# Strassen pairs in nine of eleven iterations of an up projection, with the token sums moved and the residual's row added by transfers

## The reference, cut to what matters

```python
def conv_ffn(x, w_up, b_up, w_dw, b_dw, w_down, b_down):
    h = x @ w_up + b_up                       # 1024 -> 2 * 2816
    h = causal_depthwise_conv(h, w_dw, b_dw)  # width 3
    g, val = jnp.split(h, 2, axis=-1)
    return (jax.nn.silu(g) * val) @ w_down + b_down

y = conv_ffn(x, ...)
x = layer_norm(DEEPNORM_ALPHA * x + y, norm2_g[i], norm2_b[i])   # alpha = 2 ** 0.5
```

## Time and profile before

| | before |
|---|---|
| median of 3 runs | 1028.91 us (1028.56 to 1029.22) |
| the profiled execution, its own time | 1028.89 us |
| its span, first to last instruction | 1027.0 us |
| PE busy | 1010.0 us (98%), 5091 matmuls |
| DVE busy | 839.9 us (82%) |
| ACT busy | 586.2 us (57%) |
| POOL busy | 285.3 us (28%) |
| mean granted clock of PE | 0.997 |

### The profile page before, as it was taken

The page is one execution under the profiler, slowest core; times in us unless marked ns, Lnnn a source line. Parts: engine busy times, 40 slices in busy tenths (PEclk is TensorE's granted clock), DMA queues, the critical chain, the costliest instruction groups (busy, mean ns, idle before and its releaser), DMA issues.

```text
span 1027.0 us, 14802 instructions
## 1 busy us (share of the span) xinstructions
PE 1010.0 (98%) x5091; PEld 853.8 (83%) x5091; DVE 839.9 (82%) x1154; ACT 586.2 (57%) x869; POOL 285.3 (28%) x321
## 2 busy tenths in 40 slices
PE   8999999999999999999999999999999999999997
PEld 6777788988899888888888888898888988888885
DVE  6999977698988688687895869769988867768888
ACT  6898864455665555565453443345656554456553
POOL 2988830594243100000020200049433400000001
PEclk9999999999999999999999999999999999999999
DMA  9766269379999722376555333827989963327653
GB/s 306 242 164 164 60 146 336 129 192 216 276 210 271 200 98 82 125 264 206 198 168 200 126 107 111 307 66 200 243 266 224 256 171 101 103 87 265 201 191 117
DMA packets 64440, 189.85 MB, mean 185 GB/s; under 512 B 7424, under 2 KB 8448, under 8 KB 63872
## 3 DMA queue, kind: packets, MB, share of 16 engines
q1 hardware_dynamic: 44144, 137.76, 39.6%
q0 software_dynamic: 18224, 44.05, 21.5%
q10 hardware_dynamic: 2016, 7.34, 2.1%
HBM read 178.11 MB, written 54.53 MB: 227 GB/s over the span
## 4 chain that ended last, share of the span: by engine, by line
PE 74%; DVE 10%; ACT 3%; issue 2%; DMA 1%; POOL 0%; DVEq 0%; POOLq 0%; ACTq 0%
PE ps L1981 11%; PE ps L1979 11%; PE ps L1980 11%; PE ps L2270 6%; PE ps L2272 6%; PE ps L2271 6%; PE ps L1989 4%; PE ps L1990 4%; PE ps L1991 4%; PE ps L2219 3%; PE ps L2221 3%; PE ps L2220 3%; DVE ps L1584 2%; DVE wl L1279 1%; DVE wl L1573 1%
## 5 line engine op out<-in xcount | busy, mean ns | idle before, releaser
L1979 PE MATMUL ps<-xh,wh 128*128 128x512 f32 x656 | 258.1, 394 | 0.6 <-DVE wl L1279 0.6
L1980 PE MATMUL ps<-xl,wh 128*128 128x512 f32 x656 | 255.4, 389 | 0.0
L1981 PE MATMUL ps<-xh,wl 128*128 128x512 f32 x656 | 255.3, 389 | 0.0
L784 ACT ACTIVATE wh<-raw 128x1024 fp32r<-128x1024 f32 x114 | 119.9, 1057 | 81.9 <-PE ps L2272 63.0
L1279 DVE TENSOR_TENSOR wl<-raw,wh 128x1024 fp32r<-128x1024 f32 x101 | 127.8, 1271 | 40.5 <-ACT wh L784 40.5
L1979 PEld LDWEIGHTS ps<-xh,wh 128*128 128x128 f32 x656 | 123.2, 188 | 27.2 <-issue 1.2
L1980 PEld LDWEIGHTS ps<-xl,wh 128*128 128x128 f32 x656 | 123.2, 188 | 26.1 <-issue 1.2
L1981 PEld LDWEIGHTS ps<-xh,wl 128*128 128x128 f32 x656 | 123.1, 188 | 25.8
L596 POOL TENSOR_SCALAR veps<-sqs 128x1 f32<-128x1 f32 x15 | 5.7, 383 | 496.7 <-ACT squares_down L978 377.4
L1573 DVE TENSOR_TENSOR wl<-raw,wh 128x1024 fp32r<-128x1024 f32 x70 | 89.4, 1277 | 23.6 <-ACT wh L1022 23.6
L2270 PE MATMUL ps<-wh,parts 128*128 128x512 f32 x264 | 102.7, 389 | 0.0
(11 more groups left out here) (269 smaller groups left out, 2205.6 us busy)
## 6 DMA issues: line engine op xcount, KB each, us to landing
raw<-d_weights SPq DMA_DIRECT2D x156, 512.0 KB, 4.3
raw<-summed SPq DMA_DIRECT2D x56, 512.0 KB, 4.1
summed<-d_weights POOLq DMA_DIRECT2D x88, 256.0 KB, 9.9
summed<-d_weights SPq DMA_DIRECT2D x66, 256.0 KB, 5.2
summed<-summed POOLq DMA_DIRECT2D x46, 256.0 KB, 5.6
wl<-raw POOLq DMA_DIRECT2D x4, 1024.0 KB, 7.2
wl<-raw POOLq DMA_DIRECT2D x5, 512.0 KB, 7.4
xraw<-d_x_fm SPq DMA_DIRECT2D x8, 256.0 KB, 7.1
```

Of the source, the lines that this page charges most:

```text
L784: eng.activation(split_at(u)[0], raw[:, u % RAW, :], ACT.Copy).then_inc(w_hi, 1)
L1979: eng.matmul(ps[:, bank, cols], a, xh[:, k, cols], start=(k == 0), stop=False)
L1980: eng.matmul(ps[:, bank, cols], a, xl[:, k, cols], start=False, stop=False)
L1981: mm = eng.matmul(ps[:, bank, cols], b, xh[:, k, cols], start=False, stop=(k == KD - 1))
```

## The change

- Strassen iterations are 1 to 9 instead of 2 to 6, in both layers. Iterations 0 and 10 stay regular. `first_strassen` moves from iteration 1 to iteration 0.
- The token sums move from rows 7 to 10 of all eight slots to rows 2 to 9 of four slots (`T_SLOTS`), those of the split hidden tiles. Those splits are put off: the regular iteration 0 and the Strassen iterations only make `n5` (`difference`), and iteration 10 splits rows 0 to 4 and 5 to 9 in two blocks of each of two tensors (`highs` on ACT, `lows` on DVE, 1280 columns each) and makes `s2` in two blocks (`sums_of`).
- The second two `token_parts` of the first Strassen iteration come behind its first `started` and `taps`.
- The early units and the normalisation's scratch tiles move to other slots.
- The residual of the feed-forward parts: ACT divides the bias row by ALPHA (in the first slot of iteration 0), POOL adds it to the four residual tiles by accumulating transfers behind `summed_weights`, and the first additions of the down projection multiply by ALPHA. `residual` on DVE stays in the gated MLP alone.

```diff
-S_FROM, S_TO = 2, 7
+S_FROM, S_TO = 1, 10
+T_SLOTS = (0, 1, 3, 6)
+S_ROWS, TF_ROWS, TH_ROWS = slice(0, 2), slice(2, 6), slice(6, 10)
+CHUNKS = (slice(0, S_TO // 2), slice(S_TO // 2, S_TO))
...
             summed_weights(layer)
+            eng.wait_ge(br_ok, layer + 1)
+            for t in range(NT):
+                eng.dma_start(res[:, t, :], brow[:, :], accum_op=ALU.add).then_inc(res_add, 16)
...  (ACT)
+            def highs(c):
+
+                ahead(KQ - 1, c)
+                if c == 1:
+                    eng.wait_ge(pr, 2 * S_TO + layer * KH)
+                if c in (1, 2):
+                    rows = CHUNKS[c - 1]
+                    for h, f in ((a11h, a11), (a12h, a12)):
+                        eng.activation(h[:, rows, :], f[:, rows, :], ACT.Copy).then_inc(h_hi, S_TO // 2)
+
-            regular(0, lambda c: his([u0 + c + LEAD] if c else []), in_banks)
             regular(S_FROM - 1, first_strassen, in_banks)
             strassen(S_FROM, True, lambda: token_parts((3, 2)))
             with eng.Fori(S_FROM + 1, S_TO - 1) as i:
                 strassen(i, True)
             strassen(S_TO - 1, False)
...
+            regular(KQ - 1, highs, in_sbuf, True)
...  (DVE)
+            def difference(i):
+
+                eng.wait_ge(pr, i * 2 + (layer * KH + 2))
+                eng.tensor_tensor(n5[:, bass.ds(i, 1), :], a21[:, bass.ds(i, 1), :], a22[:, bass.ds(i, 1), :],
+                                  ALU.subtract).then_inc(a_sum, 1)
+
+            def low(i, q):
+
                 eng.wait_ge(h_hi, i * 2 + (q + layer * KH + 1))
...
+            def lows(k):
+
+                rows = CHUNKS[k]
+                eng.wait_ge(h_hi, layer * KH + S_TO * (k + 1))
+                for l, f, h in ((a11l, a11, a11h), (a12l, a12, a12h)):
+                    eng.tensor_tensor(l[:, rows, :], f[:, rows, :], h[:, rows, :].bitcast(f32), ALU.subtract).then_inc(h_lo, S_TO // 2)
...
+                    product(i, q, accs)
+                    if last:
+                        low(i, q)
+                difference(i)
...
+            def last_tiles(c):
+
+                ahead(KQ - 1, c)
+                if c in (1, 2):
+                    lows(c - 1)
+                if c == 3:
+                    eng.wait_ge(h_lo, layer * KH + S_TO)
+                    sums_of(0, S_TO // 2, S_TO)
+
+            regular(KQ - 1, last_tiles, in_sbuf, True)
+            eng.wait_ge(h_lo, (layer + 1) * KH)
+            sums_of(S_TO // 2, KQ, S_TO // 2 + KQ)
...
-                    add(0, 0, p1, 1.0)
-                    add(1, 0, p1 + 1, 1.0)
+                    eng.wait_ge(res_add, 16 * NT * (layer + 1))
+                    add_first(0, p1)
+                    add_first(1, p1 + 1)
...  (PE)
-                eng.wait_ge(h_lo, layer * KH + max(2 * i + 1, 2 * (S_TO + 1)))
+                eng.wait_ge(h_lo, layer * KH + max(2 * i + 1, 2 * S_TO))
```

More of the change, by code:

```diff
@@ L210, in build_trunk @@
     a22h, a22l = slot_of(parts, 6), slot_of(parts, 7)
[L212 to L221, removed]
+    sum4h, sum4l, v2h, v2l = [parts[:, i, S_ROWS, :].rearrange("p k n -> p (k n)") for i in T_SLOTS]
+    t_f = [made[:, i, TF_ROWS, :] for i in T_SLOTS]
+    t_l = [parts[:, i, TF_ROWS, :] for i in T_SLOTS]
+    t_h = [parts[:, i, TH_ROWS, :] for i in T_SLOTS]
+    t_part = [made[:, i, TH_ROWS, :] for i in T_SLOTS]
     p16 = place("p16", [P, 2, HALF], f32, s0 + 8192)
@@ L1058, in high, with regular @@
                 eng.activation(h[:, bass.ds(i, 1), :], f[:, bass.ds(i, 1), :], ACT.Copy).then_inc(h_hi, 1)
-            def regular(i, split, accs):
+            def regular(i, split, accs, last=False):
                 for q in range(2):
@@ L1121, in first_strassen @@
             def first_strassen(c):
-                ahead(S_FROM - 1, c)
+                if c:
+                    his([u0 + c + LEAD])
+                if c == 0:
+                    eng.wait_ge(bo_in, 16 * (2 * layer + 1))
+                    eng.activation(brow[:, :], brow[:, :], ACT.Copy, scale=1.0 / ALPHA).then_inc(br_ok, 1)
                 if c == 3:
@@ L1701, in ffn_up @@
             strassen(S_TO - 1, False)
[L1702 to L1709, removed]
-            eng.tensor_tensor(s2[:, late_rows, :], n5[:, late_rows, :], a11[:, late_rows, :], ALU.subtract).then_inc(a_sum, NS)
-            regular(S_TO + 1, lambda c: ahead(S_TO + 1, c), in_sbuf)
-            residual(2 * layer + 1)
-            with eng.Fori(S_TO + 2, KQ) as i:
-                regular(i, lambda c: ahead(i, c), in_sbuf)
+            def last_tiles(c):
[8 more added lines that the diff above has]
+            sums_of(S_TO // 2, KQ, S_TO // 2 + KQ)
         def mean_of(n, t):
@@ L1760, in add, with add_first @@
                                          accum_out=sums[:, t, h:h + 1] if whole else None).then_inc(c_rd, 1)
+            def add_first(t, bank):
+                part = res[:, t, 0:HALF]
+                eng.scalar_tensor_tensor(out=part, in0=part, scalar=ALPHA, in1=ps[:, bank, :], op0=ALU.mult, op1=ALU.add).then_inc(c_rd, 1)
             def shared_sum(t):
@@ L2245, in strassen_units @@
                 part(x_bank, wh[:, three, first], wl[:, three, first], b_t[2], False).then_inc(w_used, 1)
-            with eng.Fori(1, S_FROM) as i:
-                for c in range(4):
-                    regular_unit(i, c)
             for c in range(2):
@@ L2256, in ffn @@
                 strassen_units(i)
-            with eng.Fori(S_TO, KQ) as i:
-                for c in range(4):
-                    regular_unit(i, c)
+            for c in range(4):
+                regular_unit(KQ - 1, c)
             p1, p2, p5, p6, p3, p7, p4 = products_at(n)
```

61 lines of the change are left out of this document (26 added, 35 removed).

## The result

| | before | after |
|---|---|---|
| median of the runs | 1028.83 us | 1071.91 us (1068.42 to 1077.62, 4 runs) |
| ratio, 95% interval | | 1.0421 [1.039, 1.0453] |
| profiled execution, its span | 1027.0 us | 1068.2 us |
| mean granted clock of PE | 0.997 | 0.984 |

The account below looks back on a forecast made before the run. PE streaming bounds the kernel (98% busy), DVE (82%) not far behind. New waits 22.7 us, less 4.7 of old waits and 7.0 of work saved, give +11.0 on 1028.89: 1039.9 us, range 1026 to 1050.

Parts of the forecast that it names:

- The work saved: PE's matmuls in four more Strassen iterations of each layer: 8 x 0.87 = 7.0 us less, sure to 0.2 us.
- The first pair: Strassen's start, one iteration earlier: PE waits 7.3 us in layer 0, 7.5 in layer 1; bounds 4.0 to 9.0.
- The walk of DVE's queue: DVE up to the first pair: second split ends 209.5, token parts 221.8, `difference` 224.4, first split of the sums 225.6 us.
- The first rival: Queue at the start shorter than walked, work saved wins: 1025.7 us, chance 0.17.
- my estimate of 9.5 us from the rule: Start's wait if each of DVE's nine operations waits a whole 1.27 us POOL operation, not 1.0; not used in the sum.
- The weights that arrive late: The two iterations after the first pair, late `raw` slots 2 and 3: 2.7 + 0.9 us in layer 0, 1.3 in layer 1.
- 1 to 3 us more: Added arrival time for three copies (768 KB) standing between the loads of slots 2 and 3.
- The third rival: Weights stay late for longer, POOL's transfers holding 12 us of arrival until near 264 us: 1051.6 us, chance 0.15.
- The residual at nothing: Residual moved from DVE to ACT and POOL's transfers: no gain and no cost.
- The end: End of the up projection, PE waiting for `h_lo` of 20: 1.5 us in each layer, bounds 0 and 3.
- the next weight part at T + 38: At the end, T being the end of the last pair: when the next weight part is needed, no wait counted.

Follow-up runs that it names:

- e8: Changed kernel with Strassen from iteration 2, residual transfers after the last Strassen pair, tile 20 split behind both blocks: 1018.7 us, ratio 0.9912; again 1021.2 us, 0.9918.
- e6: Kernel of e4, with PE doing 36 transposes into an unread bank before its wait in pair 1: 1048.03 us, ratio 1.0184.
- e5: Kernel of e4, with token sums made of the high parts alone, 8 POOL operations instead of 20: 1029.65 us, one time.
- e7: Changed kernel, with SP's three copies behind unit 10 issued one load earlier, not between slots 2 and 3: 1047.39, then 1048.58 us, ratio 1.0193.
- e4: Changed kernel, with POOL's weight sums begun only when PE is through four Strassen pairs of the layer: 1046.5 us, ratio 1.0188.
- e2: Changed kernel, with Strassen pairs from iteration 2 on instead of 1: 1034.02 us, ratio 1.0049.
- e9: Changed kernel with the edits of e1, e3 and e4 together, Strassen still from iteration 1: 1037.5 us, ratio 1.0087.
- e1: Changed kernel, with each layer's four residual transfers issued only when PE is through its Strassen pairs: 1065.49 us, ratio 1.0364.
- e3: Changed kernel, with ACT and DVE splitting tile 20 only behind both blocks of `highs` and `lows`: 1058.25 us, ratio 1.028.

## Why the prediction was right in its sign and wrong in its size

**The work saved** was right: an undisturbed pair is 10.04 us, 7.0 us in all. e8, with three quarters of it (5.2 us) and without before's late pairs (6.6), is 9.7 us shorter in span, and 1.4 of the 2.1 us missing from that sum stand in its own late pairs.

**The first pair** was nearly right: 7.3 and 7.5 forecast, 8.7 and 9.9 measured, inside its bounds of 4.0 to 9.0 in layer 0 and above them in layer 1. The walk of DVE's queue held within a microsecond: token parts done at 221.03 (forecast 221.8), the first split begins at 223.79 (forecast 224.4). What it missed is that this split, too, stood beside POOL's last operation: 2.29 us and not 1.13. The first wait is 4.64 and not 3.75, the clock fell in it, and the waits for `kept` are 0.30 and 0.60 and not 2.25 and 1.25. So the waits make 5.5 of the 8.7 us and not 7.3, and the lower clock, which the sum doesn't have, makes 3.1. That the sum comes near all the same is not luck: e6 shows that it hardly depends on the clock, since DVE's queue sets when the pair ends, and of the 1.4 us that are missing in layer 0 the longer split is 1.1. The first rival (the queue is shorter) is wrong, and e5 shows why it could not be: the queue is shorter only where POOL is silent.

The rule of the Trainium skill that I weighed (SBUF — State Buffer, Who interferes with whom: two SBUF inputs on DVE and a GpSimd read of SBUF exclude each other for the whole instruction) agrees with this trace in kind: each of DVE's operations there waits, and none does in e5, where POOL is done. In the moved slot DVE starts one operation in each 1.70 us on average (208.05 to 216.56, five of them), between the 1.6 by which I walked and the 1.87 (0.6 + 1.27) of full turns. Against e5, the waiting is 1.0 to 1.1 us for each of the seven moved operations and the split behind them, so the rows' 1.0 was the better figure. That my estimate of 9.5 us from the rule lies between what the two layers measured is no proof of it, since a part of both is the lower clock.

**The weights that arrive late** is the step that failed most: 4.9 forecast in both layers, 18.8 measured. The mechanism was right, and the place. The size of one row was not: "1 to 3 us more" for the three copies between the loads of slots 2 and 3. By the walk slot 3 lands 13 to 15 us behind the last split; it landed 19.7 behind it (227.3 to 247.0), and e7 gives the copies' part as 8.5 us of arrival. I had priced 768 KB as if the queue were free, while beside POOL's sums a load on it lands in 9.3 us instead of 3.3 (medians of after and e4). Once PE was behind a late slot 3, the lateness lasted over four iterations of layer 0, falling 8.2 (gap and pair), 2.5, 0.65, 0.5. The third rival named this, with 10.4 us as its price; its time, 1051.6, was too low also because the next term lay outside it and the end stood in it with 3.0 for 3.7.

**The residual at nothing** was wrong: 7.0 us. The cover that I named, "an iteration where PE doesn't wait", is cover for the instructions of DVE that leave. The transfers needed cover of their own: their queue's neighbours are the loads of slots 2 and 3, which in a Strassen iteration are issued only when the split of the sums is done, and by the prediction's own walk (18.9 of 20.95) have 2 us to spare there. I priced the collision of the transfers with the down projection and not the one with the loads at 345 us. The rows showed how loads fare beside accumulating transfers, and I used them for the start only.

**The end**: 1.5 forecast in each layer, 3.7 measured. The first wait, 1.78, came where and why the walk said. The second, 1.93, I excluded with "the next weight part at T + 38". DVE's queue behind the late blocks holds also the weights' low parts, four in a row from 452.75 (4.62 us), and PE needs the first of them at its fourth down unit, at 452.1 us, 32 behind the end of the last pair, because a down unit here is 12 matmuls of 0.227 us, 2.73, and not the twice of that by which I placed the later deadlines.

The four terms give 3.7 + 13.9 + 7.0 + 4.4 = 29.0 of the 30.2 us that the span is above the forecast. From the rest, 1.2, goes what the prediction had too small in before, 1.9 (it took off the two waits, 4.7, and the late pairs cost 6.6), and to it comes 3.5 behind the end's waits, less 0.5 ahead of the first pair, which no run explains, but for the 1.9 of the last transfer. Two of the four, 20.9 us, are one error: I asked of each transfer what waits for it, and not what it stands in front of or beside.

## What to carry to other kernels

Price a transfer by the loads it runs beside and in front of, not by who waits for it: here 2 MB of residual additions and 768 KB of copies in each layer, for which nothing waited at that time, cost 7 us and, beside the sums, 15 us. Where a later iteration's loads can be issued only by a split of the same iteration, any delay of that split goes round the loop and fades slowly, so give the first round more slack than one undisturbed round needs. And before moving vector work ahead of an iteration, look at what GpSimd does at that time; seven cheap operations moved by one iteration turned 10.05 us into 18.7, and starting one iteration later (e2, 38 us) gave more than all other repairs together (e9, 34).

## What was not expected of the hardware

The granted clock of PE. In the kernel before, PE waits 2.34 us in the first pair of each layer, for the same copy. Behind the wait of layer 0 the clock stayed at 1.00; behind that of layer 1 it was 0.50 (1.2 GHz) for 3.4 us, and the pair takes 14.11 us where layer 0's takes 12.59. The prediction took the two for equal. The stretches of before, columns as in e4's row above (the granted clock is the last but two):

```profile
247.50:252.00 4.50, 4.46 (x38) 4.49 (x38) 4.19 (x6) 2.07 (x5) 2.19 (x3) 1.00 1.10 292
738.30:741.60 3.30, 3.30 (x18) 3.30 (x17) 3.27 (x5) 1.88 (x4) 1.42 (x2) 0.50 1.08 282
```

In after it was 0.50 for 3.4 to 10.2 us at a time, in or behind the waits of 4.64 and 3.46 us in layer 0 and of 4.91 and 2.60 us in layer 1. A wait of 1.93 us at the end left it at 1.00 in after and was followed by 0.50 in e1. So the length of the wait alone does not say whether the clock falls. Two stretches of after:

```profile
225.40:232.00 6.60, 5.56 (x24) 5.30 (x25) 6.57 (x8) 4.67 (x7) 6.34 (x8) 0.50 0.85 109
252.30:255.50 3.20, 3.20 (x18) 3.20 (x17) 3.09 (x5) 1.94 (x3) 1.65 (x2) 0.52 1.12 197
```

In the first of them the matmuls of 256 columns stand 0.21 us apart instead of 0.12, which makes 3.1 of the 8.7 us of pair 1 (its waits are 5.5). In e6 pair 1 of layer 0 at full clock was no shorter, because the next thing that PE needed came from DVE and ACT anyway. That a load of 512 KB lands in anything from 3.1 to 17.4 us, by what else is under way, is the larger surprise. It is also the likely reason, not tested by itself, why kernels that differ by a few microseconds of phase differ by more than their edit: e3 and after by 4.8 us in pairs 6 and 7, e6 and e4 by 5.3 in one pair 7. What in the transfers makes the delay, their bytes, their packets or the accumulation, no run here tells apart.
